# Moving two weight splits, a group of attention loads and one wait in a decoder layer's interleaving table

## The reference

```python
h = rmsnorm(x, p['norm_mix_g'])
z = jnp.einsum('btd,de->bte', h, p['w_in'])
gq, gk, gv, gg, glr, dq, dk, dv = jnp.split(z, _split_points(), axis=-1)
...
S_new, o_g = gla_fn(q_g, k_g, v_g, log_a)
o_g = rmsnorm(o_g.astype(x.dtype), p['gla_norm_g']) * jax.nn.silu(gg.reshape(B, T, H_GLA, DV_GLA))
q_d = rmsnorm(dq.reshape(B, T, H_DIFF, 2, DH_DIFF), p['q_norm_g'])
k_d = rmsnorm(dk.reshape(B, T, H_DIFF, 2, DH_DIFF), p['k_norm_g'])
...
o_d = attn_fn(q_d, k_d, v_d, lam)
o_d = rmsnorm(o_d, p['diff_norm_g']) * (1.0 - lambda_init)
x = x + jnp.einsum('bte,ed->btd', mix, p['w_out'])
h2 = rmsnorm(x, p['norm_ffn_g'])
u = jnp.square(jax.nn.relu(jnp.einsum('btd,df->btf', h2, p['w_up'])))
x = x + jnp.einsum('btf,fd->btd', u, p['w_down'])
```

## Time and profile before

| | us |
|---|---|
| three runs | 1367.66, 1365.40, 1366.08 (median 1366.08) |
| the profiled execution | 1367.66 |
| its span in the profile | 1365.9 |
| busy: PE, DVE, ACT, POOL | 1345.8, 894.1, 577.7, 401.4 |
| mean granted clock of PE | 0.997 |

### The profile page before, as it was taken

One profiled execution on the slowest core, in us unless ns is written; L12 is line 12 of the kernel. 1 busy time (PEld: TensorE's weight loads), 2 busy tenths in 40 slices (PEclk: granted clock), 3 DMA queues, 4 the chain that ended last, 5 costly groups with the idle time before them and its releaser, 6 DMA issues.

```text
span 1365.9 us, 23927 instructions
## 1 busy us (share of the span) xinstructions
PE 1345.8 (99%) x8605; PEld 1122.1 (82%) x8605; DVE 894.1 (65%) x1619; ACT 577.7 (42%) x1075; POOL 401.4 (29%) x395
## 2 busy tenths in 40 slices
PE   9999999999999999999999999999999999999998
PEld 8778778777777777777776777667999999999998
DVE  6469567746758776748656574534466665877785
ACT  7563333416545554622325241322454454344532
POOL 3648334445515445333000000000342212332030
PEclk9999999999999999999999999999999999999999
DMA  9467734453255573656677575873555564132311
GB/s 327 120 192 226 230 122 150 154 155 117 86 178 180 175 274 123 226 178 233 196 253 255 169 252 167 300 254 109 176 203 180 176 232 165 53 109 109 109 32 63
DMA packets 125544, 239.30 MB, mean 175 GB/s; under 512 B 13601, under 2 KB 46658, under 8 KB 125426
## 3 DMA queue, kind: packets, MB, share of 16 engines
q1 hardware_dynamic: 116226, 213.64, 47.6%
q10 hardware_dynamic: 9200, 24.13, 5.2%
HBM read 197.64 MB, written 40.09 MB: 174 GB/s over the span
## 4 chain that ended last, share of the span: by engine, by line
PE 85%; DVE 6%; DMA 3%; ACT 2%; issue 2%; SPq 1%; POOL 1%; ACTq 0%; DVEq 0%; POOLq 0%
PE ps L87 23%; PE ps L89 22%; PE ps L88 22%; PE ps L1553 2%; PE ps L1372 2%; PE ps L3372 2%; PE ps L1590 2%; DMA kr<-in_cache_k 2%; DVE sd L3124 1%; PE ps L1574 1%; DVE wl L828 1%; POOL kr L3137 1%; DVE uw_l L2079 1%; PE ps L423 1%; PE ps L1414 1%
## 5 line engine op out<-in xcount | busy, mean ns | idle before, releaser
L3137 POOL TENSOR_TENSOR kr<-kr,qb 128x512 f32<-128x512 f32 x128 | 178.9, 1404 | 205.9 <-DMA kr<-in_cache_k 148.4
L87 PE MATMUL ps<-x2hB,uw_h 128*128 128x264 f32 (+1 forms) x512 | 145.2, 284 | 0.7 <-DVE x2lB L2923 0.7
L88 PE MATMUL ps<-x2lB,uw_h 128*128 128x264 f32 (+1 forms) x512 | 144.7, 283 | 0.0
L89 PE MATMUL ps<-x2hB,uw_l 128*128 128x264 f32 (+1 forms) x512 | 144.5, 282 | 0.0
L87 PE MATMUL ps<-part_h,fh 128*128 128x264 f32 (+1 forms) x448 | 127.8, 285 | 0.0
L89 PE MATMUL ps<-part_h,fl 128*128 128x264 f32 (+1 forms) x448 | 127.0, 284 | 0.0
L88 PE MATMUL ps<-part_l,fh 128*128 128x264 f32 (+1 forms) x448 | 126.8, 283 | 0.0
L2908 DVE TENSOR_TENSOR xt<-xt,ps 128x264 f32<-128x264 f32 (+1 forms) x224 | 87.3, 422 | 35.8 <-PE ps L89 35.6
L3124 DVE TENSOR_REDUCE sd<-kr 128x8 f32<-128x512 f32 x128 | 84.9, 675 | 38.3 <-POOL kr L3137 38.3
L87 PE MATMUL ps<-uh,dh 128*128 128x512 f32 x256 | 105.0, 410 | 3.0 <-DVE xt L2227 2.3
L87 PE MATMUL ps<-x2hA,uw_h 128*128 128x512 f32 x256 | 105.5, 412 | 0.0
(11 more groups left out here) (392 smaller groups left out, 3415.1 us busy)
## 6 DMA issues: line engine op xcount, KB each, us to landing
kr<-in_cache_k SPq DMA_DIRECT2D x128, 256.0 KB, 3.2
raw_up<-in_w_up_units SPq DMA_DIRECT2D x64, 512.0 KB, 4.8
vr<-in_cache_v SPq DMA_DIRECT2D x128, 256.0 KB, 3.5
raw_dn<-in_w_down SPq DMA_DIRECT2D x32, 512.0 KB, 6.5
raw_dn<-in_w_down ACTq DMA_DIRECT2D x32, 512.0 KB, 5.3
raw<-in_w_in_units SPq DMA_DIRECT2D x23, 512.0 KB, 5.6
raw_up<-in_w_out_units SPq DMA_DIRECT2D x16, 512.0 KB, 4.1
kept_up_low<-uw_l SPq DMA_DIRECT2D x14, 512.0 KB, 5.9
```

The lines of the kernel that those rows point to most:

```text
L87: pe.matmul(out, lh, rh, start=first and n == 0, stop=False, skip_group_check=onto)
L88: pe.matmul(out, lh, rl, start=False, stop=False, skip_group_check=onto)
L89: ins = pe.matmul(out, ll, rh, start=False, stop=last and n == len(ks) - 1, skip_group_check=onto)
L3137: pool.tensor_tensor(k[:, :], k[:, :], qb[v // PAGES][:, :], ALU.mult).then_inc(k_multiplied, 1)
```

## The change

Seven edits.
- The table of splits gives unit 11 to group 22 instead of 21, and at group 22 the side jobs' steps now stand ahead of the split.
- The late splits move from the end of groups 54 and 55, behind the second tick's steps, to a place right behind the group's evacuation, on ACT and DVE.
- The first step of `loadA` comes two ticks later and waits for one more semaphore, go_made.
- POOL no longer waits, ahead of the products 33 to 57, for the sum of the product before.
- `mixload` comes three ticks earlier.

```diff
-    table = {1: [4], 2: [5], 9: [6], 11: [7], 12: [8, 9], 21: [10, 11], 24: [12], 27: [13],
+    table = {1: [4], 2: [5], 9: [6], 11: [7], 12: [8, 9], 21: [10], 22: [11], 24: [12], 27: [13],
...
             evacuate(g)
+            if g in (START["gg"] + 3, START["gg"] + 4):
+                m["late"]["scalar"](act, g - START["gg"] - 3)
...
             if ticks_of(g) == 2:
                 beside(TICK[g] + 1)
-            if g in (START["gg"] + 3, START["gg"] + 4):
-                m["late"]["scalar"](act, g - START["gg"] - 3)
...
-            units_first = g in (START["gv"] - 3, START["dk"] + NTILE)
+            units_first = g in (START["gv"] - 3, START["gv"] - 2, START["dk"] + NTILE)
...
                 if x[1] == 2:
                     gkq_sample(g)
+            if g in (START["gg"] + 3, START["gg"] + 4):
+                m["late"]["vector"](dve, g - START["gg"] - 3)
...
             if ticks_of(g) == 2:
                 beside(TICK[g] + 1)
-            if g in (START["gg"] + 3, START["gg"] + 4):
-                m["late"]["vector"](dve, g - START["gg"] - 3)
...
         if part == 0:
-            for x in ("o_summed", "state_summed"):
+            for x in ("o_summed", "state_summed", "go_made"):
                 sp.wait_ge(sem(x), CHUNKS)
...
                 pool.wait_ge(page_in[i], n)
-                if 33 <= v < 58:
-                    pool.wait_ge(k_used, v)
...
-        put("loadA", [t0 - 4, t0 + 1])
+        put("loadA", [t0 - 2, t0 + 1])
...
-        put("mixload", [t0 + 120 + 2 * i for i in range(4)])
+        put("mixload", [t1 + 57 + 2 * i for i in range(4)])
```

## The result

The changed kernel is slower: 1372.94 us in the median of 20 runs (1370.03 to 1378.25), against 1365.74 for the kernel before (20 runs, 1362.79 to 1373.44). The ratio is 1.0054, 95% interval 1.0042 to 1.0066, or about 7.4 us. The forecast was 1366.3 with a range up to 1370.0, so the time is outside it. The profiled execution of the changed kernel took 1378.11, which is near the longest of the twenty; its trace shows where time is lost, and the comparison of medians how much of it is usual.

A forecast was written before the change was run, and what follows sets the result against it. TensorE was taken as the bound, busy 1345.8 of 1365.9 us. Against the profiled 1367.66, −1.1 − 1.7 − 0.4 + 1.5 + 0.3 = −1.4 gave 1366.3 us, range 1363.0 to 1370.0.

The forecast's parts named there:

- The wait of POOL: POOL's products without the k_used wait: moved meetings with DVE work cost 0 to 2.5 us, taken as 0.
- gain of 0.4 at 259: TensorE's 0.38 us wait at 259.42 for a split beside a product goes: −0.4 us.
- rival D: POOL's products and DVE's two-input operations draw each other out, gain at 163 not reached: 1368.6 us, chance 0.12.
- loadA: Attention's first loads, 278 to 300 us: TensorE waits 1.3 for qt, 0 to 0.2 behind; +1.5, ends 0 and 3.1.
- rival C: SP's queue: kt and qt land late, TensorE stands 2.9 us, a half-clock stretch adds 1.7: 1369.6 us, chance 0.22.
- The late splits: At 357 to 372 us: the second split delays p0a by 1.05 us, TensorE loses 0.3, at most 0.5.
- Unit 11's split: At 131 to 163 us: the 1.14 wait goes, a new one of 1.5 comes, SP's chain gains 1.1: −1.1 us.
- The stretch at 165.8: The half-clock stretch behind TensorE's 1.90 us wait at 163.33 goes: −1.7 us, between −1.7 and 0.
- L1372 of 163.33: TensorE starts it 1.1 us earlier, at 162.2, since sums and SP's stores come earlier; 0.4 of standing left.
- mixload: Loads of rowsB three ticks earlier, hidden with 38 us to spare: 0, ±0.3 us.

The follow-up runs named there:

- e2_burst: Kernel before, with POOL's wait on k_used gone for the products of pages 53, 54 and 55 alone: 1366.83 us, ratio 1.0002 (0.9986 to 1.0018).
- e10_load_wait: Kernel before, with the added condition on go_made for the first attention loads, at their old tick: 1375.64 against 1367.68 us, ratio 1.0062.
- e6_regate4: Changed kernel, with POOL's wait on k_used put back for pages 52 to 55 alone: 1370.93 us, ratio 1.0033 to the kernel before.
- e4_split: Kernel before, with only unit 11's split moved to group 22, behind the side steps: 1364.74 against 1366.56 us, ratio 0.9989 (0.9977 to 1.0000).
- e12_two_back: Changed kernel, with POOL's wait on k_used and the attention's first loads put back as before: 1365.83 us, ratio 0.9987 to the kernel before.
- e13_split_mixload: Kernel before, with unit 11's split behind the side steps and rowsB's loads three ticks earlier: 1363.83 against 1365.56 us, ratio 0.9982.
- e1_gate: Kernel before, with only POOL's wait on k_used removed for all 25 products: 1371.15 against 1366.56 us, ratio 1.0021 (1.0003 to 1.0038).
- e9_free4: Kernel before, with POOL's wait on k_used gone for pages 52 to 55: 1371.71 against 1367.68 us, ratio 1.0036 (1.0021 to 1.0052).
- e7_load_ticks: Kernel before, with only the tick of the attention's first loads later, no added condition: 1370.56 against 1366.73 us, ratio 1.0041.
- e3_loada: Kernel before, with only the attention's first loads later and waiting for go_made too: 1369.96 against 1366.56 us, ratio 1.0034.

## Why the prediction was wrong, step by step

**The wait of POOL: the step that failed most.** It was priced at 0, with an end of 2.5 us, and a gain of 0.4 at 259. That gain came (the wait there is gone), but the step treated each freed product as one meeting with one DVE operation at 0.9 to 1.1 us. What the wait did before was to keep products apart. In the changed kernel's trace POOL ends a product at 256.97, stands 7.03 us for DVE's zsum (L873) and then does two small operations (L766, L767) up to 267.36. Pages 52 to 54 have long landed by then and page 55 lands at 267.18, so without the wait four products run in a row, and DVE's L1263 pays for the row: 5.49 us instead of 0.48, 3.1 at TensorE, and a stretch at half clock, 1.5. The rival D had the mechanism and a price of 1.1. Measured alone: +0.21% (0.03 to 0.38), and +0.36% (0.21 to 0.52) for the four pages by themselves.
One reading of the earlier trace rows was wrong too. The prediction takes 1.22 for a split without a product beside it and 2.32 for one with it. But the first of the two splits in the earlier trace rows (125.96 to 127.18) had a product beside it too, from 126.26 on; the split kept its 1.22, and the product took 2.07. The second split began while that product ran, ended at 129.41, and it was the next product that took 2.26. So the trace before already showed that a meeting can draw out either side, DVE's operation or POOL's product.
On the rule of the Trainium skill ("GPSIMD Engine Reference", § 1 Specifications) the runs agree in kind: L1263 and L1694, two inputs in SBUF, are held (4.2 us instead of 0.28, 1.33 instead of 0.22); L1279 and the sums, with one input there, are not (2.18 for four beside the row in e2_burst, 2.15 before; a sum 0.69 beside a product).

**loadA: the mechanism was right, the size wrong.** Forecast were a wait of 1.3 for qt and 0.2 behind it, +1.5. Two terms were too small. The landing: taken as 5.0 us, it was 5.9 in the changed kernel (296.18 to 302.07) and 6.2 in the run alone (290.28 to 296.48), the upper part of the earlier trace rows. In the four traces with page 58 and the query row issued just ahead, the first qt took 5.7 to 6.3; without them it took 5.1 before and 4.2 in e10_load_wait. That speaks for those two as the cause, but no run isolates it. And the clock: the 1.7 us were kept for rival C. Wait, clock and the later p0a came to 2.2, 1.5 and 0.9 in the trace; alone it cost +0.34% (0.15 to 0.53), 4.6 us, nearly the 4.8 of that rival, though the run's own trace shows only the wait. The added condition showed no cost, and the reason given, that the page in front has it too, fits. Without that page in front it costs most of all (e10_load_wait).

**The late splits: +0.3 forecast, a wait of 1.2 in each trace that has them.** The shift of the chain by 1.05 was right for the split itself (stat at 371.67 in the run alone, behind a split of 1.23). What was missed is that the shifted chain meets a product of POOL at L1694, another 1.1. In time the part alone is +0.10% (−0.05 to +0.26), not clear of no change.

**Unit 11's split: its waits as forecast, its gain in time not clear of the noise.** The wait of 1.14 at 131 went, as forecast, and the new one came: 2.64 in the changed kernel and 2.78 in e6_regate4, 1.75, 1.13 and 1.69 in e4_split, e12_two_back and e13_split_mixload, where 1.5 was taken. In the first two the clock fell with it (136.5 and 137.4), which was not forecast. The stretch at 165.8 went, as forecast, with the reserve told at e4_split. The step in between, that L1372 of 163.33 starts 1.1 us earlier, fits but is not shown: L1372 starts at 163.9 in the mean of the five traces with the split behind the side steps (161.3 to 165.5) and at 165.0 in the mean of the nine with it as before (163.3 to 167.4), a spread larger than the step. Alone: −0.11% (−0.23 to 0), where −2.8 us (0.2%) with the clock, or −1.1 without, follow from the steps.

**mixload** was hidden, as forecast, as far as the four traces beside the changed kernel's own show.

**The chances.** C and D were held to be alternatives, at 0.22 and 0.12, each with the rest as forecast. The costs measured apart add up, so nothing made them alternatives, and both came. The sum of both, 1366.3 + 3.3 + 2.3 = 1371.9, is nearly what was measured, and in part by luck: D's 2.3 are a meeting of 1.1 and a gain at 163 that isn't reached, not a row with a wait of 3.1 and a fall of the clock.
**The range.** It left out what its own terms allow. The prediction says that the terms' ends give 1364.6 to 1368.0; added up against the same 1367.66, the ends it states (0 and 0 at 163 and 165.8, +2.5 for POOL's wait, +3.1 for loadA, +0.5 for the late splits) reach 1373.8, and 1363.7 at the lower side. The measured 1372.94 lies within those, so the range was narrower than its working.

## What to carry to other kernels

A wait that looks like a needless order between two engines may be spacing their work: before it is taken out, look for the place where the freed engine has a backlog (here POOL waited and worked elsewhere for 10.4 us, up to 267.36, while pages came in), and price the whole row against the DVE operations with two inputs in SBUF that stand there, not one meeting. Not each of them pays for the whole row, as the split in e2_burst shows; which one does was found here only by running it. A transfer issued anew behind others is priced at the upper end of its landing times, and what stands behind a waiting DMA on the same queue, a store that frees a slot above all, is part of the price. Where several edits each risk a wait, their losses add; the range has to hold the case in which two come together.

## What was not expected of the hardware

A two-input operation of DVE can be held rather than slowed: in the changed kernel the first of the two L1263 ran from 267.04 to 271.22, while three products ended one after another at 268.6, 269.8 and 271.1 with no gap between them; e1_gate (4.00) and e9_free4 (4.17) repeat it. An operation of one element (L1694) is held for a whole product too. But the splits that met products back to back got their turn behind the first of them (2.32 at 127.1 before, 1.48 at 275.3 in e2_burst), and the next product took 2.3. Why L1263 let three pass and a split only one is open.

The clock does not fall with every standing of a given length. It fell next to waits of 1.34 (e10_load_wait, at 164.5), 1.69 (e7_load_ticks, at 159) and 1.90 (before, at 163), and did not after 2.62 at 296.5 in e3_loada, 2.07 at 298.4 in e7_load_ticks and 1.75 at 136.5 in e4_split. The same wait, 2.24 and 2.61 at the same place in the changed kernel and in e6_regate4, had a stretch at half clock. A stretch of 3.4 us cost 1.4 to 1.7 us, and three traces have one of 6.8 us (e2_burst, e9_free4, e10_load_wait). So one trace shows what a stretch costs there, but not whether the median run has it. The mean clock of each execution tells more: its median is 0.997 for the changed kernel and 0.999 for the kernel before as it ran beside the experiments; 0.002 of the span is about 2.7 of the 7.4 us.
